# The scans' constants and first logarithms made in the projection stage, and the order of turns and side copies inside the scan

## The reference

```python
def forget_log(fx, lb, shape):
    f = lb + (1.0 - lb) * jax.nn.sigmoid(fx.astype(jnp.float32))
    return jnp.log(f).reshape(shape)

def hgrn2_scan(q, logf, inp, s0):
    ...
    k = -jnp.expm1(logf)
    ...
    def step(S, xs):
        qc, lc, kc, ic = xs
        b = jnp.cumsum(lc, axis=2)
        rel = jnp.where(mask[:, :, None], b[:, :, :, None, :] - b[:, :, None, :, :], -jnp.inf)
        A = jnp.einsum('bhtk,bhtsk,bhsk->bhts', qc, jnp.exp(rel), kc)
        o = jnp.einsum('bhts,bhsv->bhtv', A, ic) + jnp.einsum('bhtk,bhkv->bhtv', qc * jnp.exp(b), S)
        bl = b[:, :, -1:, :]
        S = jnp.exp(bl[:, :, 0, :])[..., None] * S + jnp.einsum('bhsk,bhsv->bhkv', kc * jnp.exp(bl - b), ic)
        return S, o
```

## Time and profile before

| | |
|---|---|
| three runs | 7143.82, 7139.61, 7142.99 us; median 7142.99 |
| the profiled execution's own time | 7144.25 us |
| its span in the trace | 7142.5 us |
| busy share of the span | PE 80%, DVE 56%, POOL 39%, ACT 27% |
| the forward scan of the first layer | starts near 318.9 us, its last DVE copy ends at 482.1 us |
| the stage after it | starts near 493.1 us |

### The profile page before, as it was taken

One profiled execution on the slowest core, in us unless ns is written; L12 is line 12 of the kernel. 1 busy time (PEld: TensorE's weight loads), 2 busy tenths in 40 slices (PEclk: granted clock), 3 DMA queues, 4 the chain that ended last, 5 costly groups with the idle time before them and its releaser, 6 DMA issues. The chain is left out here.

```text
span 7142.5 us, 97163 instructions
## 1 busy us (share of the span) xinstructions
PE 5678.9 (80%) x37784; PEld 4039.4 (57%) x37784; DVE 4007.6 (56%) x8102; ACT 1914.8 (27%) x3637; POOL 2760.7 (39%) x2928
## 2 busy tenths in 40 slices
PE   4877999879487787778787789997875777878776
PEld 3866999759333333333367679996773333333332
DVE  2266342264677677776634472424546677767776
ACT  1356211141122222222215452112302222222221
POOL 0211000010277777777602200001005777777774
PEclk8998999999799999999989899998988999999998
DMA  5100121102799999999930111110158999999998
GB/s 225 44 35 24 72 83 71 49 27 92 303 408 406 404 408 405 405 405 407 395 140 9 41 52 71 71 71 26 51 207 322 406 405 404 407 406 401 409 398 323
DMA packets 424143, 1658.76 MB, mean 232 GB/s; under 512 B 48136, under 2 KB 67272, under 8 KB 409420
## 3 DMA queue, kind: packets, MB, share of 16 engines
q0 software_dynamic: 368640, 1342.34, 47.4%
q1 hardware_dynamic: 53598, 304.86, 11.2%
q10 hardware_dynamic: 1440, 5.24, 0.2%
HBM read 1637.40 MB, written 17.48 MB: 232 GB/s over the span
## 5 line engine op out<-in xcount | busy, mean ns | idle before, releaser
L1834 PE MATMUL ex_ps_y<-early,peer_small 128*128 128x512 f32 x5120 | 2390.8, 613 | 754.3 <-DMA early<-in_peer_v,ex_index 754.2
L1834 PEld LDWEIGHTS ex_ps_y<-early,peer_small 128*128 128x128 f32 x5120 | 941.0, 193 | 2123.1 <-DMA early<-in_peer_v,ex_index 1274.1
L1717 DVE CUSTOM_DVE_ANT_0 ring<-ring,ex_ps_h 128x1024 f32<-128x1024 f32 x1280 | 1518.8, 1218 | 817.6 <-DMA ring<-in_peer_u,ex_index 802.8
L1592 POOL DMA_INDIRECT ring<-in_peer_u,ex_index x1280 | 1220.1, 953 | 759.7 <-issue 303.6
L1592 POOL DMA_INDIRECT early<-in_peer_v,ex_index x1280 | 1226.5, 958 | 425.0 <-issue 377.5
L1787 ACT ACTIVATE peer_small<-ident,ex_w 128x128 f32<-128x128 f32 x1280 | 448.3, 393 | 951.1 <-PE ex_ps_y L1834 951.1
L738 POOL TENSOR_TENSOR att_qs<-att_q,ring 128x512 f32<-128x512 f32 x16 | 20.2, 1263 | 1108.5 <-DMA att_lam_in<-in_lam 951.6
L237 PE MATMUL conv_ps<-h_high,conv_wh 128*128 128x320 f32 x1024 | 317.2, 310 | 8.2 <-DVE conv_wl L135 8.2
L1777 ACT ACTIVATE ex_act<-ex_dot 128x16 f32<-128x16 f32 x80 | 17.2, 216 | 1141.2 <-DVE ex_dot L1717 1141.2
L237 PE MATMUL conv_ps<-h_high,conv_wl 128*128 128x320 f32 x1024 | 317.1, 310 | 0.0
L237 PE MATMUL conv_ps<-h_low,conv_wh 128*128 128x320 f32 x1024 | 317.0, 310 | 0.0
(11 more groups left out here) (329 smaller groups left out, 12313.5 us busy)
## 6 DMA issues: line engine op xcount, KB each, us to landing
ring<-in_w_in SPq DMA_DIRECT2D x54, 2048.0 KB, 7.8
ring<-in_mod_w SPq DMA_DIRECT2D x16, 2048.0 KB, 15.9
ring<-in_w_branch SPq DMA_DIRECT2D x12, 2048.0 KB, 7.8
early<-in_mod_w SPq DMA_DIRECT2D x12, 2048.0 KB, 19.2
ring<-in_peer_u,ex_index POOLq DMA_INDIRECT x1280, 8.9
early<-in_peer_v,ex_index POOLq DMA_INDIRECT x1280, 9.1
mod_w<-in_mod_w SPq DMA_DIRECT2D x8, 2048.0 KB, 24.7
room<-in_peer_wq SPq DMA_DIRECT2D x16, 1024.0 KB, 16.1
```

The costliest lines, as they stand in the source:

```text
L1592: nc.gpsimd.indirect_dma_start(rows[slot], None, table, bass.IndirectOffsetOnAxis(ap=index[n % 4][:, s:s + 1], axis=0)).then_inc(arrived[s ...
L1717: V.tensor_tensor_reduce(out=row, in0=row, in1=ps_h[:], scale=1.0, scalar=0.0, op0=ALU.mult, op1=ALU.add, accum_out=dot[n % 2][:, s:s + 1] ...
L1834: last = nc.tensor.matmul(ps_y[n % 2][:, c:c + 512], diag[s % DIAGS], v_row[s % V_SLOTS][:, c:c + 512], start=s == 0, stop=s == TOPK - 1)
```

## The change

- The loads of `levels`, `suffix`, `cmask` and `bmask` go from the scan's SP list to that of the projections ahead of it, in front of the weights. Levels and suffix are staged in parts of `kk` that are still free; ACT rounds them behind its first two splits (`scalar_first`).
- The first group's clamp (`pool_after_tile`), logarithm and high part (`scalar_after_half`, behind the half before the last) and low part (`vector_last`) are made in the projections, so the scan's POOL loop and `logs`, `low` begin with group 1.
- `turn(g+1)` stands behind the second `span_sums` of group g and not behind the first; on ACT, `rests` and the side copies move one unit later and are split 5, 4, 6 and not 2, 5, 4, 4.
- In group 0, ACT makes 7 side copies behind the first exponential and DVE the other 8 at the scan's start; `logs(1)` stands behind the second exponential.
- For d = 0, SP issues the weights for `ring[0]` before the new state's store, and no longer behind it.

```diff
@@ -266,6 +275,7 @@
                 steps = Steps(act, act_steps)
                 split(0)
                 split(1)
+                beside.scalar_first(act)
...
                     if half_of[r] + 2 < n_halves:
                         dve.wait_ge(tile_done, done_through[r])
                         split(half_of[r] + 2)
+                beside.vector_last(dve)
...
                     if isinstance(job, Job) and job.after_on == "gpsimd":
                         pool.wait_ge(slot_free[t % 4], t // 4 + 1)
                         job.after(step, m, e)
+                    beside.pool_after_tile(pool, step, t)
...
 class BoundsBeside(Beside):
 
-    names = ("bounds",)
+    names = ("bounds", "consts", "clamped", "logs", "loghigh", "rest")
...
+        self.first, self.n_halves = kk[:, block, 0:D // 2], halves
+        self.spare = [kk[:, b, D // 2:D] for b in (0, 1, 2)]
 
     def load(self, sp):
+        T, d, head = self.T, self.d, self.head
         for j in range(2):
             sp.dma_start(self.lb[:, j, :], self.rows(j)).then_inc(self.S[0], 16)
+        levels = T["levels"][d].rearrange("p a t -> p (a t)")
+        for j in range(2):
+            sp.dma_start(self.spare[j], levels[:, j * (D // 2):(j + 1) * (D // 2)]).then_inc(self.S[1], 16)
+        sp.dma_start(self.spare[2][:, 0:P], T["suffix"][d]).then_inc(self.S[1], 16)
+        sp.dma_start(head.cmask[:], T["cmask"][d]).then_inc(self.S[1], 16)
+        sp.dma_start(head.bmask[:], T["bmask"]).then_inc(self.S[1], 16)
...
+    def scalar_first(self, act):
+        act.wait_ge(self.S[1], 16 * 5)
+        for j in range(2):
+            act.activation(self.head.levels[:, j * (D // 2):(j + 1) * (D // 2)], self.spare[j], ACT.Copy)
+        act.activation(self.head.suffix[:], self.spare[2][:, 0:P], ACT.Copy)
+
+    def pool_after_tile(self, pool, step, t):
+        if t != self.first_ready:
+            return
+        pool.wait_ge(step.sem, step.n)
+        self.nc.gpsimd.tensor_scalar(self.head.lf[:], self.first, TINY, None, ALU.max).then_inc(self.S[2], 1)
+        pool.wait_ge(self.S[2], 1)
+        self.nc.gpsimd.tensor_scalar(self.first, self.first, -1.0, 1.0, ALU.mult, ALU.add).then_inc(self.S[5], 1)
+
+    def scalar_after_half(self, act, i):
+        if i != self.n_halves - 2:
+            return
+        lf = self.head.lf
+        act.wait_ge(self.S[2], 1)
+        act.activation(lf[:], lf[:], ACT.Ln).then_inc(self.S[3], 1)
+        act.wait_ge(self.S[3], 1)
+        act.activation(self.head.lf_high[:], lf[:], ACT.Copy).then_inc(self.S[4], 1)
+
+    def vector_last(self, dve):
+        dve.wait_ge(self.S[4], 1)
+        low_part(self.nc, self.head.lf_low[:], self.head.lf[:], self.head.lf_high[:])
...
+                beside = BoundsBeside(nc, T, d, lb, lambda j: T["lb_rows"][d, bass.ds(l, 1), j, :].to_broadcast([P, D]),
+                                      kk, 0 if d == 0 else NB - 1, head, 2 * len(jobs))
+                beside.first_ready = sum(2 * job.tiles for job in jobs[:-1]) - 1
+                projections(nc, f"rf{d}", jobs, ring, beside)
+                loop.close()
+                scan(nc, l, T, d, q_t, i_tok, kk, o_tok, ring, ident, w_in(T, l, (RFB, RG)[d]), head)
...
         def span_item(n):
-            return 1 + n + min((n + G - 1) // G, GROUPS - 1)
+            return 1 + n + min((n + G - 2) // G, GROUPS - 1)
 
         def turn_item(g):
-            return span_item(G * (g - 1)) + 1 if g else 0
-
-        with stage(nc, "sc_in", "sc_cast", "sc_gate", "sc_ln", "sc_high", "sc_low", "sc_span", "sc_exped", "sc_turned", "sc_kdec",
+            return span_item(G * (g - 1) + 1) + 1 if g else 0
+
+        SIDES = 2 * LEVELS + 1
+
+        def side_parts(g, i):
+
+            view = sides[g % 2].rearrange("p (h a t) -> p h a t", h=G, a=XW)
+            keys = k_tr[g % 3][:].rearrange("p (h t) -> p h t", h=G)
+            queries = q_t[:, (g % 2) * G:(g % 2 + 1) * G, blocks[g // 2] * P:(blocks[g // 2] + 1) * P]
+            if i == 2 * LEVELS:
+                return view[:, :, LEVELS, :], queries
+            a, half = i % LEVELS, (lower, upper)[i // LEVELS]
+
+            def halves(t):
+                return t.rearrange("p h (blk two sub) -> p h blk two sub", two=2, sub=1 << a)[:, :, :, half, :]
...
-                sp.dma_start(xs[0][:, 0, :], T["levels"][d].rearrange("p a t -> p (a t)")).then_inc(loaded, 16)
-                sp.dma_start(xs[1][:, 0, 0:P], T["suffix"][d]).then_inc(loaded, 16)
-                sp.dma_start(cmask[:], T["cmask"][d]).then_inc(loaded, 16)
-                sp.dma_start(bmask[:], T["bmask"]).then_inc(loaded, 16)
                 sp.dma_start(state[:], T["state"][one, d].rearrange("a p n -> (a p) n")).then_inc(loaded, 16)
-                sp.wait_ge(s_done, (blocks.index(CTX_BLOCK) + 1) * BLOCK_PAIRS)
-                sp.dma_start(T["new_state"][one, d].rearrange("a p n -> (a p) n"), state_ctx).then_inc(s_out, 16)
+                def new_state():
+                    sp.wait_ge(s_done, (blocks.index(CTX_BLOCK) + 1) * BLOCK_PAIRS)
+                    sp.dma_start(T["new_state"][one, d].rearrange("a p n -> (a p) n"), state_ctx).then_inc(s_out, 16)
+
+                if blocks[0] == CTX_BLOCK:
+                    new_state()
                 sp.wait_ge(x_done, PAIRS - GP)
                 sp.wait_ge(carry_ready, PAIRS - GP)
                 sp.dma_start(ring[0][:], then).then_inc(s_out, 16)
+                if blocks[0] != CTX_BLOCK:
+                    new_state()
                 sp.wait_ge(s_out, 32)
...
-                    pe.wait_ge(low_done, g + 1)
-                    pe.wait_ge(rest_ready, g + 1)
+                    if g:
+                        pe.wait_ge(low_done, g)
+                        pe.wait_ge(rest_ready, g)
...
-                        if n % G == 0 and n // G + 1 < GROUPS:
+                        if n % G == 1 and n // G + 1 < GROUPS:
...
-                pe.wait_ge(loaded, 16 * 5)
-                pe.wait_ge(zeroed, 1)
-                pe.wait_ge(cast, 2)
                 turn(0)
                 for n in range(4):
                     ahead(n)
+                pe.wait_ge(zeroed, 1)
                 for q in range(PAIRS):
...
-                for g in range(GROUPS):
-                    if g:
-                        pool.wait_ge(low_done, g)
+                for g in range(1, GROUPS):
+                    if g >= 2:
+                        pool.wait_ge(low_done, g - 1)
...
-                act.wait_ge(loaded, 16 * 5)
-                act.activation(levels[:], xs[0][:, 0, :], ACT.Copy).then_inc(cast, 1)
-                act.activation(suffix[:], xs[1][:, 0, 0:P], ACT.Copy).then_inc(cast, 1)
-                act.wait_ge(cast, 2)
-                logs(0)
-                logs(1)
                 rests(0)
-                side(0, 0, 2 * LEVELS + 1)
                 for n in range(UNITS):
                     g = n // G
                     exps(n)
+                    if n == 0:
+                        side(0, 0, LEVELS - 1)
+                        act.activation(*side_parts(0, LEVELS - 1), ACT.Copy).then_inc(sides_done, 1)
+                    if n == 1:
+                        logs(1)
                     if g + 1 < GROUPS:
-                        if n % G == 0:
+                        if n % G == 1:
                             rests(g + 1)
-                            side(g + 1, 0, 2)
-                        elif n % G == 1:
-                            side(g + 1, 2, 7)
+                            side(g + 1, 0, 5)
                         elif n % G == 2:
-                            side(g + 1, 7, 11)
+                            side(g + 1, 5, 9)
                             if g + 2 < GROUPS:
                                 logs(g + 2)
-                        else:
-                            side(g + 1, 11, 15)
+                        elif n % G == 3:
+                            side(g + 1, 9, SIDES)
 
             @block.vector
             def _(dve):
@@ -1301,12 +1367,13 @@
...
                 V.memset(ps_a[:, OFF:OFF + 2 * P], 0.0).then_inc(zeroed, 1)
-                low(0)
+                for i in range(LEVELS, SIDES):
+                    step(V.tensor_copy(*side_parts(0, i)))
+                decayed(0)
+                times(0)
                 low(1)
-                decayed(0)
-                dve.wait_ge(loaded, 16 * 5)
-                times(0)
                 carrying(0)
                 for q in range(PAIRS):
                     g = q // GP
```

66 lines of the change are left out of this document (37 added, 29 removed).

## The result

The changed kernel takes 7105.04 us, the median of 5 runs (7101.42 to 7111.67); the kernel before, timed beside it, takes 7139.61 (7135.89 to 7143.82, 5 runs). The ratio is 0.9949 with a 95% interval of [0.9937, 0.9961]. That is faster by about 35 us, and above the predicted range of 7045 to 7098. The profiled run took 7111.67 (span 7109.4), against 7144.25.

What follows compares the result with a forecast made beforehand. The prediction saw latency at scan starts, a two-pair cycle waiting on ACT's exponentials, and late weights at the forward scan's end. Gains of 15.6 us a scan, 62.4 in four, plus 13.6 made 76.0: 7067 us, range 7045 to 7098.

Steps and rivals of the forecast that it cites:

- The start: Start of each scan: `times(0)` about 8 us and `times(1)` about 20 us in, gaining 8.7 us a scan.
- ScalarE: Activation LUTs: Table switches in the projections at about 2.66 us with drain: 0.5 us less gained a scan, a sum of 74.
- The end: End of the forward scan (d = 0): only the store is awaited, gaining 6.8 us, twice, 13.6 in all.
- The projections: Stages ahead of the scans: added work costs 0 us; about 5 us a stage if the cover were gone.
- The cycle: Two pairs in a scan's middle: 13.56 us instead of 14.06; from pair 1 to 19, 6.9 us gained a scan.
- Behind pair 16 ... DVE works without a wait, as before: ... 15.9: Last pairs of each scan, 16 to 19: 15.9 us, unchanged, with logarithms at an end.
- Slower: PE falls to the lower level in the cycle: Rival for the scans' middle: PE's clock drops, cycle 17.0 us, 88 us lost against 48 gained, 7183; chance 0.04.
- faster: Whole kernel: quicker than before, chance 0.91.
- TensorE: Matmul & The Clock Gate: PE in the cycle: transposes don't count as work for the clock, which raises the slower rival's chance a little.

Runs made afterwards that it cites:

- e1: The kernel before with only SP's order at the forward scan's end changed, weights issued ahead of the store: 7126.56 us, ratio 0.9983.
- e2: The kernel before with only the turn moved behind the second `span_sums` and the side copies behind the exponentials: 7167.60 us, ratio 1.0033.
- e4: The changed kernel with 64 useless small matmuls once a scan, at pair 1 ahead of the turn: 7114.63 us, ratio 0.9967.
- e5: The changed kernel with 32 useless small matmuls once a scan, at pair 1 ahead of the turn: 7109.85 us, ratio 0.9952.
- e10: The kernel of e2 with eight useless 256-column matmuls ahead of each turn's wait from the second group on: 7124.25 us, ratio 0.9972.
- e3: The changed kernel with turn and side copies back in their old places and `low(1)` ahead of `times(0)`: 7090.62 us, ratio 0.9934.
- e6: The changed kernel with eight useless 256-column matmuls ahead of each turn's wait from the second group on: 7073.44 us, ratio 0.9901.
- e11: The kernel of e6 with 48 useless small matmuls added at pair 1: 7083.77 us, ratio 0.9920.

## Why the prediction missed

**The start: right.** 8.7 a scan were forecast and 9.1 to 10.2 came, because the first turn ran at the higher clock level and not at the lower one that the sum took (0.90 us from its start at 318.88 to the first `span_sums` at 319.78, against 1.73), and `times(0)` came at 6.8 and not 8.1. The second turn took its 1.73 (328.27 to 330.00). The mechanism was as named: PE waits for the low half, which stands behind `times(0)`. The page "ScalarE: Activation LUTs" of the Trainium skill (What ACT_TABLE_LOAD costs), by which `rests(0)` would come later, isn't borne out: from the load's start at 302.38 to the next activation at 303.67 it is 1.29 us, and the activation ahead of the load ended at 302.36, which leaves no room for a drain.

**The end: right.** 6.8 forecast, 7.2 measured in the profile, 12 us for two in e1.

**The projections: right.** They cost nothing; the covers held as worked out.

**The cycle: the step that failed.** "Sum 13.56, against 14.06" was right as a sum of durations: undisturbed cycles take 6.37 + 7.23 = 13.6. What failed is the step from it to "From pair 1 to pair 16 are then seven cycles and one 6.45: 101.4", that is, taking every cycle of a scan as undisturbed; it measured 108.2 to 110.3. With it failed "Behind pair 16 ... DVE works without a wait, as before: ... 15.9": there the path runs over PE as well, and it measured 19.0 to 22.1. In the old order PE's slack took up the disturbances. PE's timeline of the kernel before has a wait for `scan_w` at `pairs` in each cycle from pair 4 on, 1.0 to 2.4 us long. The first row below is of the first scan, the second, with a stall, of the last:

```profile
418.62 0.52 PE L1165 MATMUL scan_ps_a<-scan_x 128*32 128x32 f32 x38 [2.35 <-DVE scan_w L1338]
...
4180.09 0.27 PE L1197 MATMUL scan_ps_o<-rec_i,scan_w 128*128 128x128 f32 x1 [1.58 <-issue]
```

The two pairs around that stall take 14.35 us, against 14.06. There is one such stall in each scan, of 0.6 to 1.6 us. The change takes the slack away and puts PE on the path, with a wait of up to 2.07 us ahead of the stretch that has to be fast. e2 shows the loss by itself; e4, e5 and the count by pieces show that the stalls belong to the list; e10 against e2 shows the clock's part where no stall stands. Stalls with what follows them are the larger share, 35 us of excess against 14.

**The rivals.** "Slower: PE falls to the lower level in the cycle" had one of the two mechanisms, with 0.04 for its chance; no rival had the late instructions. Its price for a cycle, 17.0, was near (9.76 + 6.37 = 16.1), but only part of the cycles fall; falls and stalls together cost the changed kernel 46 us against the forecast. The argument against it, that the clock was 0.97 today and that the work would be packed tighter, overlooked that a mean over a stretch says nothing about where the wait will stand. For the cycle even the direction was wrong: alone, the move of the turn is a loss (e2), and the gain comes from the other two parts (e3). The forecast "faster" came true through them alone. That transposes don't count as work for the clock, by "TensorE: Matmul & The Clock Gate" (Part 4) of the same skill, is not told apart by any run here, since the fillers were ordinary matmuls.

**What stays open.** Why some pieces come late and others, fetched as often, don't; why there are fewer stalls with fillers of 256 columns (4 or 5 intervals hold one in e6, e10 and e11, 9 or 10 in the other kernels with the new turn place); and how the 46 us divide exactly, since a clock fall stands behind the long stalls and the two add up in one interval (10.73 is 7.23, 2.0 of stall, and 1.5 of slower matmuls and smaller things). Outside the scans the kernels differ by some microseconds in either direction in stages whose code is the same, and nothing here was tried on that.
